# The gated attention's share of the mixing product computed inside the masked attention

## The reference

```python
y_gla = o_gla * silu(ggate)                  # gated linear attention, 384 wide
o_dsa = dsa_mixer(dq, dk, dv, qi, ki, wi, rel_bias)   # masked attention, 6 heads of 64
y_dsa = o_dsa * silu(dgate)                  # 384 wide
y_pool = pool_mixer(pu, ...) * silu(pgate)   # 256 wide
y = concatenate([y_gla, y_dsa, y_pool], axis=-1)
x = x + einsum('btc,cd->btd', y, w_out[l])
```

## Time and profile before

| | us |
|---|---|
| median of 3 runs | 3885.74 (3884.17 to 3886.39) |
| the profiled execution | 3876.22 |
| its span in the trace | 3874.4 |
| TensorE busy over the span | 3518.0 (91%) |
| VectorE busy | 1371.8 (35%) |
| ScalarE busy | 724.2 (19%) |
| GpSimd busy | 251.5 (6%) |

### The profile page before, as it was taken

The page is one execution under the profiler, slowest core; times in us unless marked ns, Lnnn a source line. Parts: engine busy times, 40 slices in busy tenths (PEclk is TensorE's granted clock), DMA queues, the critical chain, the costliest instruction groups (busy, mean ns, idle before and its releaser), DMA issues. The chain is left out here.

```text
span 3874.4 us, 31095 instructions
## 1 busy us (share of the span) xinstructions
PE 3518.0 (91%) x11334; PEld 1693.8 (44%) x11334; DVE 1371.8 (35%) x2302; ACT 724.2 (19%) x1456; POOL 251.5 (6%) x342
## 2 busy tenths in 40 slices
PE   7996889999984999999999998696799988999998
PEld 2444433444432444444444443344444686444443
DVE  4882721793233111111010111635445376311111
ACT  2102301012111101101010110315344355010000
POOL 0000021000001000000000001000000375000000
PEclk8995599999997999999999998798899899999999
DMA  6860027211126999999999994212323002112120
GB/s 211 283 230 15 22 98 287 87 65 65 65 91 257 357 402 392 399 398 395 402 388 402 390 401 175 88 65 87 113 87 101 27 26 77 66 65 87 65 87 22
DMA packets 209230, 710.90 MB, mean 183 GB/s; under 512 B 16847, under 2 KB 27488, under 8 KB 174310
## 3 DMA queue, kind: packets, MB, share of 16 engines
q1 hardware_dynamic: 182348, 632.40, 43.3%
q0 software_dynamic: 13584, 48.44, 3.4%
q10 hardware_dynamic: 13194, 28.69, 2.0%
HBM read 655.59 MB, written 53.89 MB: 183 GB/s over the span
## 5 line engine op out<-in xcount | busy, mean ns | idle before, releaser
L1928 PE MATMUL bank<-moe_gu,all_hT 128*128 128x512 f32 x1088 | 471.0, 593 | 0.0
L2126 DVE TENSOR_SCALAR all_hT<-bank 128x512 f32<-128x512 f32 x51 | 35.3, 691 | 855.2 <-PE bank L1934 700.1
L1384 PE MATMUL bank<-all_hT,early_w 128*128 128x512 f32 x768 | 332.3, 595 | 5.9 <-ACT all_hT L546 5.9
L1928 PEld LDWEIGHTS bank<-moe_gu,all_hT 128*128 128x128 f32 x1088 | 207.2, 191 | 260.6 <-issue 260.6
L1966 PE MATMUL bank<-moe_dn,moe_rows 128*128 128x512 f32 x544 | 237.9, 595 | 4.2 <-ACT moe_rows L2046 4.2
L1947 PE MATMUL bank<-moe_gu,all_hT 128*64 128x512 f32 x1088 | 236.5, 592 | 0.4 <-issue 0.4
L2762 PE MATMUL bank<-all_hT,hin_w 128*128 128x512 f32 x512 | 222.4, 597 | 14.1 <-DMA hin_w<-in_w_in_dram 14.1
L1384 PEld LDWEIGHTS bank<-all_hT,early_w 128*128 128x128 f32 x768 | 146.6, 191 | 191.2 <-issue 189.7
L1276 PE MATMUL bank<-all_hT,late_w 128*128 128x512 f32 x512 | 221.9, 596 | 5.9 <-ACT all_hT L546 5.9
L1276 PE MATMUL bank<-b_up,late_w 128*128 128x512 f32 x512 | 220.0, 592 | 1.7 <-PEq L1242 1.7
L1426 DVE SCALAR_TENSOR_TENSOR b_conv<-conv_ya,all_table,b_conv 128x512 f32<-128x512 f32 x240 | 159.4, 742 | 0.0
(11 more groups left out here) (606 smaller groups left out, 4099.1 us busy)
## 6 DMA issues: line engine op xcount, KB each, us to landing
moe_gu<-in_w_gu_dram SPq DMA_DIRECT2D x136, 2048.0 KB, 13.8
moe_dn<-in_w_dn_dram SPq DMA_DIRECT2D x68, 2048.0 KB, 13.2
early_w<-in_w_in_dram SPq DMA_DIRECT2D x13, 2048.0 KB, 7.8
expert_rows<-b_z POOLq DMA_DIRECT2D x49, 512.0 KB, 20.1
mods_w<-in_w_mod_dram SPq DMA_DIRECT2D x48, 512.0 KB, 4.8
mods_w<-in_ada_w_dram SPq DMA_DIRECT2D x48, 512.0 KB, 5.1
hin_w<-in_w_in_dram SPq DMA_DIRECT2D x10, 2048.0 KB, 8.4
late_w<-in_w_up_dram SPq DMA_DIRECT2D x8, 2048.0 KB, 8.9
```

The lines of the kernel that those rows point to most:

```text
L1384: mm = nc.tensor.matmul(bank(n)[:], w[:, k, (n % 4) * P:(n % 4 + 1) * P], hT[:, k, :], start=(k == 0), stop=(k == KT - 1))
L1928: mm = nc.tensor.matmul(B[bank][:], xb2[:, k, :], gu[:, q, kk, col:col + HALF], start=(k == 0), stop=False)
```

## The change

The products of `y_gla` with `w_out` leave `mix_out`. They are made inside `dsa_attend`, in B[7], and VectorE adds them into `xT` there. B[7] was the third logit bank, so the logits use two banks. `mix_gla(j)` stands behind the logits in unit j: of each output tile m, unit 3m makes two products, units 3m+1 and 3m+2 one each. `add_mix(m)` stands in VectorE's iteration 3m+4, between the maximum of that unit and the normalising of the one before, the last one behind the loop. `mix_out` keeps five products per tile. The piece counts of the stream change with it, and `dsa_attend` issues one load more.

```diff
-def dsa_attend(core, to, ident, spare, bias, flip, windows, pick, y, pool_mix):
+def dsa_attend(core, to, ident, spare, bias, flip, windows, pick, y, pool_mix, xT, y_gla):
...
-        logit_bank = lambda i: B[(0, 1, 7)[i % R]]
+        logit_bank = lambda i: B[i % 2]
+        stream = core.early
+        base = stream.base()
...
             pool_mix.load(sp)
+            stream.load(sp, 1)
...
-                if i >= R:
-                    pe.wait_ge(biased, i - R + 1)
+                if i >= 2:
+                    pe.wait_ge(biased, i - 1)
...
-            for i in range(R):
-                logits_of(i)
+            w_gla = stream.take(pe)
+
+            def mix_gla(j):
+                m, part = divmod(j, 3)
+                if part == 0 and m:
+                    pe.wait_ge(mixed, m)
+                for h in ((0, 1), (2,), (3,))[part]:
+                    mm = nc.tensor.matmul(B[7][:], w_gla[:, h, m * P:(m + 1) * P], y_gla[:, h, :], start=(h == 0),
+                                          stop=(h == GLA_H - 1))
+                if part == 2:
+                    mm.then_inc(stream.product, 1)
+
+            logits_of(0)
+            logits_of(1)
...
-                if j + R < N:
-                    logits_of(j + R)
+                if j + 2 < N:
+                    logits_of(j + 2)
+                mix_gla(j)
...
+            def add_mix(m):
+                dve.wait_ge(stream.product, base + m + 1)
+                nc.vector.tensor_tensor(xT[:, m, :], xT[:, m, :], B[7][:], ALU.add).then_inc(mixed, 1)
+
...
+                if i >= 4 and i % 3 == 1:
+                    add_mix((i - 4) // 3)
...
+            add_mix(KT - 1)
             pool_mix.scale(dve)
...
-    return [(by(0, 384, GLA_DV), KT), (by(384, 768, P), 0), (by(768, D, P), 0)]
+    return [(by(0, 384, GLA_DV), KT), (by(384, 768, P), KT), (by(768, D, P), 0)]
...
-    parts = [(y_gla, h, GLA_DV) for h in range(4)] + [(y_dsa, k, P) for k in range(3)] + [(y_pool, k, P) for k in range(2)]
+    parts = [(y_dsa, k) for k in range(3)] + [(y_pool, k) for k in range(2)]
...
-            stream.load(sp, 3)
+            stream.load(sp, 2)
```

More of the change, by code:

```diff
@@ L970, in dsa_attend @@
         L, pr, prT = spare[:, 0:R], spare[:, R:2 * R], spare[:, 2 * R:2 * R + 2]
-        logit_bank = lambda i: B[(0, 1, 7)[i % R]]
-        (logits, biased, peaked, exped, weights, turned, turned_copied,
+        logit_bank = lambda i: B[i % 2]
+        stream = core.early
+        base = stream.base()
+        (logits, biased, mixed, peaked, exped, weights, turned, turned_copied,
          attended, step, gated, flipped, flip_copied) = sems(
-            nc, ctx, *(f"att_{s}" for s in ("logits", "biased",
+            nc, ctx, *(f"att_{s}" for s in ("logits", "biased", "mixed",
                                             "peaked", "exped", "weights", "turned", "turned_copied",
@@ L1155, in mix_pieces, with mix_out @@
     by = lambda lo, hi, p: w_out[lo:hi].rearrange("(k p) n -> p k n", p=p)
[L1156 to L1159 removed]
+    return [(by(0, 384, GLA_DV), KT), (by(384, 768, P), KT), (by(768, D, P), 0)]
+def mix_out(core, xT, y_dsa, y_pool):
     nc = core.nc
     B = core.bank
[L1163 removed]
+    parts = [(y_dsa, k) for k in range(3)] + [(y_pool, k) for k in range(2)]
     with ExitStack() as ctx:
@@ L1171, in _ @@
         def _(sp):
-            stream.load(sp, 3)
+            stream.load(sp, 2)
         @block.tensor
         def _(pe):
-            pieces = [stream.take(pe) for _ in range(3)]
+            pieces = [stream.take(pe) for _ in range(2)]
             weights = [(w, j) for w in pieces for j in range(w.shape[1])]
             for m in range(KT):
-                for i, (y, k, rows) in enumerate(parts):
+                for i, (y, k) in enumerate(parts):
                     w, j = weights[i]
-                    mm = nc.tensor.matmul(B[m][:], w[:, j, m * P:(m + 1) * P], y[0:rows, k, :], start=(i == 0),
+                    mm = nc.tensor.matmul(B[m][:], w[:, j, m * P:(m + 1) * P], y[:, k, :], start=(i == 0),
                                           stop=(i == len(parts) - 1))
@@ L1219, in first_block @@
             pool_mix = PoolMix(core, inner, to, a["pool_w"][0], a["pool_scale"][0], y_pool)
-            dsa_attend(core, to, ident, hT, bias, flip, windows, pick, y_dsa, pool_mix)
-        mix_out(core, xT, y_gla, y_dsa, y_pool)
+            dsa_attend(core, to, ident, hT, bias, flip, windows, pick, y_dsa, pool_mix, xT, y_gla)
+        mix_out(core, xT, y_dsa, y_pool)
 CONV_W, SGU_G = 31, 8
```

## The result

| | before | changed |
|---|---|---|
| median of 4 runs, us | 3884.95 (3875.01 to 3886.39) | 3922.13 (3916.87 to 3924.12) |
| ratio of the runs | 1 | 1.0101, 95% interval 1.0089 to 1.0113 |
| span of the profiled execution, us | 3874.4 | 3922.3 |

What follows compares the result with a forecast made beforehand. The prediction took a serial chain between TensorE and VectorE to bound the masked attention: +54.7 us there, less 27.4 from the mixing product, +27.3 on the 3885.7 us median, 3913.0 us. The range was 3893 to 3931 us.

Steps and rivals of the forecast that it cites:

- What went from the mixing product: Mixing product: eight output tiles each lose eight MATMUL instructions, 3.43 us per tile, 27.4 us less.
- The serial chain: Masked attention: with two logit banks, transposing, attending, logits and one VectorE iteration follow serially; 512-key periods 5.7 to 7.9 us.
- the factor 0.57: Masked attention: transposing, attending and logits at 2.4 GHz take 0.57 of their 1.2 GHz times, assumed for smaller sizes too.
- the share at 2.4 GHz: Masked attention: clock goes up and down, 2.4 GHz for 0.45 of the work; range 0.85 to 0.1.
- the prediction's own line: Masked attention's time: 154.1 us all at 1.2 GHz, less 0.45 x 48.8 for the full clock, 132 us.
- From about the second or third such unit on: Masked attention: units with four new instructions together behind logits raise the clock from about then on.
- Transfers: Weight loads: earlier loading brings no gain; uncovered, the load on SP would cost one issue, a microsecond or so.
- The additions: VectorE in the masked attention: eight of 0.72 us with gaps, seven in the chain, 5.0 us; the eighth hidden.
- (a): Masked attention: first dense pair lifts the clock and it stays up; +0.5 us, 3886 us; chance 0.09.
- (b): Masked attention: clock never lifted except at the end; +49.3 us, 3935 us; chance 0.09.
- (c): Masked attention: logits early enough, so TensorE's own work bounds the stage; about -29 us, 3857 us; chance 0.04.

Runs made afterwards that it cites:

- two banks alone: Kernel before with two logit banks in place of three, no new products, no additions: 3942.87 us, ratio 1.0148, stage 132.2 us.
- the run with early pairs and two banks: Changed kernel with additions behind the weights' multiplication and new products two per unit, first two ahead of the first transposition: 3886.64 us, 1.0006 to the kernel before.
- the run above: Changed kernel with 128-row query and key operands in place of 96 rows in the new products: stage 121.0 us, 70.4 at 2.4 GHz; kernel time not comparable.
- the run that moved them: Changed kernel with seven of VectorE's additions moved behind the weights' multiplication of the same iteration: 3909.04 us, 1.0065 to the kernel before.
- the run without the early pair: Changed kernel with three logit banks, one transposing bank, additions behind the weights' multiplication, two new products in each of units 0 to 15: 3868.38 us, 0.9960 to before.
- the run with early pairs: Changed kernel, three logit banks, one for transposing, additions behind weights' multiplication, two new products before first transposition, two in each of units 0-14: 3852.94 us, 0.9916 to before.
- the run with three banks and the additions behind: Changed kernel with three logit banks, transposing through one, and additions behind the weights' multiplication: 3874.97 us, 0.9979 to the kernel before.

## Why the prediction was right

**What went from the mixing product**: 27.4 us said, 27.6 measured.

**The serial chain** was the step on which all rested, and it held: two banks alone cost 58 us. Its sizes were right too. At 512 keys and 1.2 GHz 7.9 us had been said, and the run with two banks only has 8.03; the 1.75 us for attending had been read across the rise of the clock at 475.3, and it takes 1.89 at 1.2 GHz (514.23 to 516.12). At 2.4 GHz 5.7 had been said and the changed kernel has 5.96, with its transposing partly still at 1.2. That its first period shown above, 7.99, is so near to 7.9 is chance: it has an addition more and 128 keys less in two of its terms. At 384 keys and 2.4 GHz, where no row of before had T, A and L, the factor 0.57 gives 0.47 + 0.8 + 0.95 + 2.5 = 4.7, and the run with early pairs and two banks has 4.73:

```profile
463.33 0.55 PE L1036 MATMUL bank<-all_ident,all_hT 128*128 128x128 f32 x3 [0.63 <-DVE all_hT L1086]
...
468.06 0.55 PE L1036 MATMUL bank<-all_ident,all_hT 128*128 128x128 f32 x3 [0.63 <-DVE all_hT L1086]
```

**The term that was mis-sized is the share at 2.4 GHz**: 0.45 said, 17.0 of 146.0 us measured, 0.12. Put into the prediction's own line it gives 154.1 - 0.12 x 48.8 = 148 us, and 146.0 was measured; with 0.45 it was 132. That accounts for 16 us, 2 more than the forecast's whole error of 14 us in this stage. The measured share is almost at the lower end of the range that had been given for it, 0.1: the clock was the term that was least understood.

"From about the second or third such unit on" was wrong: the clock first rose at 506.3, behind the sixth group of four instructions. I had taken all 512-column products for the dense kind; in such a mix those with 96 rows did far less for the clock than those with 128 in the run above. The stretch that I had cited for dense work (400.2 to 403.6) had 128 rows. But 96 rows are not the reason by themselves: the first products of the mixing product before have 96 rows too (L1181 from 492.1 on), one right behind the other, and the clock rose behind them:

```profile
492.40:495.70 3.30, 3.30 (x5) 1.32 (x4) 0.00 (x0) 0.00 (x0) 0.00 (x0) 0.50 0.02 5
495.80:499.10 3.30, 3.30 (x9) 1.41 (x8) 0.00 (x0) 0.00 (x0) 0.00 (x0) 1.00 0.00 0
```

So it is those products among transpositions, attending and logits that failed to lift it.

**Transfers**: "no gain" was wrong by 3.2 us. I had looked at the transfers' landing and not at the time that SyncE takes to issue them. The barrier behind the mixing product waits for SyncE, three issues in a row take 4.2 us, and the change took one of the three away. This is the other correction, of the other sign: 14 too little, 3.2 too much, and 27.3 becomes 38, as against 37 measured. That the forecast came out only 10 us low is in part luck, since these errors have opposite signs. (The range's upper end is 3930 by its own sum, 3885.7 + 44.4, and not 3931.)

**The additions**: 5.0 us in the chain said, some 7.5 by the run that moved them, if the split above is right. VectorE waited 7.7 us for new products: 1.7 ahead of earlier additions, where 2 at most had been said, and 6.0 ahead of the last one (554.57), which the last attending (554.46 to 555.48) hides as forecast.

**The rivals.** (a), the clock that stays up, is out: TensorE was at 0.50 for the first 95 us of the stage, with no wait over 2.7 us. What the Trainium skill says there ("TensorE: Matmul & The Clock Gate", section "Why this matters for your kernels"), that continuous matmul work is enough, this stage doesn't bear out: the run without the early pair was busy for 33.47 of 33.47 us at 0.50. Against idle gaps the same section warns only where they are longer than the one here; in the run of pairs the clock fell in a wait of 2.5 us (at 409.5), and filling it won 15 us. (b) was nearer than I had thought, and (c), the faster case, had its condition right and was not this kernel: with logits early enough there is no chain, and the run with early pairs shows it, 32 us faster than before (26.5 by the traces up to the next block's projection), where (c) had said 29.

## What to carry to other kernels

Before a PSUM bank is taken from a buffer between two engines, count how many units ahead it lets the one engine run: with one fewer, work that lay side by side becomes a sum, here 58 us, while another bank of the same stage could be had for nothing (0.9998). Work that is to fill a stage of small products did best here when it was spread so that TensorE has some in every early unit and in the first wait (0.9916), with the additions that hang on it behind whatever the next unit waits for. And count what the queue of SyncE has to issue ahead of a barrier, apart from when the data lands.

## What the runs showed of the hardware

- TensorE can be busy without a pause for tens of us and stay at 1.2 GHz: 54 us in the run with three banks and the additions behind (53.98 of 54.00, below), 33.5 in the run of pairs. The changed kernel with other operands of 128 rows in place of 96 in its new products had 70 us at 2.4 GHz in place of 17.

```profile
411.50:465.50 54.00, 53.98 (x102) 23.10 (x102) 31.71 (x87) 9.97 (x38) 0.00 (x0) 0.50 0.00 0
465.60:511.00 45.40, 45.05 (x193) 23.34 (x192) 29.34 (x68) 14.12 (x33) 0.00 (x0) 1.00 0.04 11
```

- Filling a wait of 2.5 us on TensorE won 15 us of the kernel's time (pairs with and without the early one). Nearly all of it is the clock's: behind the unfilled wait stand 33.5 us at 1.2 GHz, which by the prediction's factor of 0.57 would be some 19 at 2.4 (an estimate); the pair itself takes 2.0 us.
- The third of three DMA issues in a row took 3.1 us on SyncE, where the first two took 1 us together. The three issues of the kernel before (duration in ns: least, median, most; first and last start):

```profile
L187 SPq DMA_DIRECT2D early_w<-in_w_in_dram x3: 368/574/3107, 555.9 to 556.9; - x3
```
